# A 1024-wide trunk kernel: expert down weights loaded as two neighbouring rows per partition, with the gated rows transposed in steps of two

## The reference, cut to what matters

```python
D_MODEL, D_FF, N_EXPERTS, TOP_K = 1024, 3584, 8, 2
def swiglu(h, w_gu, w_down):
    g, u = jnp.split(h @ w_gu, 2, axis=-1)
    return (jax.nn.silu(g) * u) @ w_down
...
    for e in range(N_EXPERTS):
        out = out + combine[..., e:e + 1] * swiglu(h, w_gu[e], w_down[e])
```

## Time and profile before

| what | value |
|---|---|
| median of 3 runs | 1553.64 us |
| the profiled execution's own time | 1553.86 us |
| its span in the profile | 1552.1 us |
| mean granted clock of TensorE, of 1 | 0.994 |
| TensorE busy | 98% of the span |
| VectorE, ScalarE busy | 79%, 66% |
| main DMA queue, share of 16 engines | 77.5% |

### The profile page before, as it was taken

The page is one execution under the profiler, slowest core; times in us unless marked ns, Lnnn a source line. Parts: engine busy times, 40 slices in busy tenths (PEclk is TensorE's granted clock), DMA queues, the critical chain, the costliest instruction groups (busy, mean ns, idle before and its releaser), DMA issues.

```text
span 1552.1 us, 21140 instructions
## 1 busy us (share of the span) xinstructions
PE 1516.8 (98%) x7606; PEld 1276.4 (82%) x7606; DVE 1220.1 (79%) x1014; ACT 1023.6 (66%) x935; POOL 60.4 (4%) x98
## 2 busy tenths in 40 slices
PE   8899999999899999999999999999999999999997
PEld 7688888888899888788888888888888888888885
DVE  6664555456688758898898898898898998998896
ACT  5554444354678646877777777777777777776774
POOL 2052000000000002000000000000000000001020
PEclk9999999999999999999999999999999999999999
DMA  8369755546433338999999999999999999999997
GB/s 323 120 238 413 262 179 185 190 135 186 136 114 122 110 136 302 404 384 404 364 383 390 372 366 409 365 386 389 364 388 389 365 391 388 365 391 382 392 382 309
DMA packets 166230, 476.23 MB, mean 307 GB/s; under 512 B 9152, under 2 KB 35024, under 8 KB 166176
## 3 DMA queue, kind: packets, MB, share of 16 engines
q1 hardware_dynamic: 157152, 446.73, 77.5%
q0 software_dynamic: 5888, 19.23, 3.2%
q10 hardware_dynamic: 3136, 9.54, 1.5%
HBM read 454.49 MB, written 20.97 MB: 306 GB/s over the span
## 4 chain that ended last, share of the span: by engine, by line
PE 88%; DVE 5%; ACT 3%; DMA 2%; DVEq 1%; issue 1%; SPq 0%; ACTq 0%
PE bank L770 27%; PE bank L772 27%; PE bank L771 27%; PE bank L1223 2%; DVE acc L1666 1%; DMA ring<-swa_w_qkv_in 1%; DVE w_lo L1340 1%; DMA ring<-moe_w_gu_in 1%; ACT w_hi L447 0%; DVE w_lo L1728 0%; PE bank L1210 0%; PE bank L990 0%; PE bank L795 0%; ACT xs L620 0%; ACT L629 0%
## 5 line engine op out<-in xcount | busy, mean ns | idle before, releaser
L1728 DVE TENSOR_TENSOR w_lo<-ring,w_hi 128x2048 fp32r<-128x2048 f32 x336 | 763.0, 2289 | 79.0 <-PE bank L772 71.2
L664 ACT ACTIVATE w_hi<-ring 128x2048 fp32r<-128x2048 f32 x336 | 636.3, 1920 | 151.0 <-DMA ring<-moe_w_gu_in 101.7
L770 PE MATMUL bank<-w_hi,xgT_hi 128*128 128x512 f32 x896 | 351.2, 392 | 3.7 <-DVE w_lo L1728 2.6
L772 PE MATMUL bank<-w_hi,xgT_lo 128*128 128x512 f32 x896 | 349.0, 390 | 0.0
L771 PE MATMUL bank<-w_lo,xgT_hi 128*128 128x512 f32 x896 | 348.7, 389 | 0.0
L1340 DVE TENSOR_TENSOR w_lo<-ring,w_hi 128x2048 fp32r<-128x2048 f32 (+1 forms) x84 | 190.0, 2265 | 118.2 <-ACT w_hi L447 118.1
L447 ACT ACTIVATE w_hi<-ring 128x2048 fp32r<-128x2048 f32 (+1 forms) x84 | 158.9, 1897 | 121.7 <-PE bank L772 114.1
L770 PEld LDWEIGHTS bank<-w_hi,xgT_hi 128*128 128x128 f32 x896 | 168.2, 188 | 38.8 <-DVE w_lo L1728 3.4
L772 PEld LDWEIGHTS bank<-w_hi,xgT_lo 128*128 128x128 f32 x896 | 168.2, 188 | 35.3
L771 PEld LDWEIGHTS bank<-w_lo,xgT_hi 128*128 128x128 f32 x896 | 168.3, 188 | 34.1
L770 PE MATMUL bank<-w_hi,m_hT_hi 128*128 128x512 f32 x448 | 175.8, 392 | 0.0
(11 more groups left out here) (326 smaller groups left out, 1650.9 us busy)
## 6 DMA issues: line engine op xcount, KB each, us to landing
ring<-moe_w_gu_in SPq DMA_DIRECT2D x230, 1024.0 KB, 7.3
ring<-moe_w_down_in SPq DMA_DIRECT2D x112, 1024.0 KB, 7.0
ring<-ffn_w_gu_in SPq DMA_DIRECT2D x28, 1024.0 KB, 6.4
ring<-ffn_w_down_in SPq DMA_DIRECT2D x14, 1024.0 KB, 4.9
xg_rows<-zeros POOLq DMA_DIRECT2D x36, 256.0 KB, 12.4
ring<-ssm_w_in_in SPq DMA_DIRECT2D x8, 1024.0 KB, 4.9
ring<-ssm_w_in_in SPq DMA_DIRECT2D x16, 512.0 KB, 3.8
ring<-ssm_w_in_in SPq DMA_DIRECT2D x32, 256.0 KB, 4.3
```

Of the source, the lines that this page charges most:

```text
L664: act.activation(w_hi[:, c % HI], ring[:, c % RING], ACT.Copy).then_inc(hi_ready, 1)
L770: pe.matmul(o, stat[0], mov[0], start=start, stop=False)
L772: return pe.matmul(o, stat[1], mov[0], start=False, stop=stop)
L1728: dve.tensor_tensor(w_lo[:, c % SPLIT], ring[:, c % RING], w_hi[:, c % HI].bitcast(F32), ALU.subtract).then_inc(lo_ready, 1)
```

## The change

The load of a down chunk takes another view of the weights: partition p now gets rows 256c + 2p and 256c + 2p + 1, which lie beside each other in memory, 8 KB in one piece. So place k of chunk c holds row 256c + 2p + k. The transposes are cut to match: tile a of `f` takes columns of `m_hh` two apart, from column 256 (a // 2) + a % 2, instead of 128 neighbouring ones. Tile 2c + k then has hidden column 256c + 2p + k on partition p.

```diff
                     else:
                         n = D
-                        src = block_of(moe_w_down[0, e], 2 * (c - 4 * NJ), 2, 0, D)
+                        src = moe_w_down[0, e].rearrange("(c p k) n -> p c k n", p=P, k=2)[:, c - 4 * NJ]
                     dst = ring[:, c % RING, :].rearrange("p (k n) -> p k n", n=n)
                     sp.dma_start(dst, src).then_inc(slot_loaded[c % RING], 16)
...
                     for a in range(4):
-                        ins = pe.transpose(bank[4 + f % 2][:, a * P:(a + 1) * P], m_hh[:, f % 2, a * P:(a + 1) * P],
-                                           ident[:])
+                        of_tile = m_hh[:, f % 2].rearrange("p (c n k) -> p c k n", c=2, k=2)[:, a // 2, a % 2]
+                        ins = pe.transpose(bank[4 + f % 2][:, a * P:(a + 1) * P], of_tile, ident[:])
                     ins.then_inc(m_T, 1)
```

## The result

| | before | after |
|---|---|---|
| median | 1553.44 us (12 runs) | 1556.38 us (12 runs) |
| the profiled execution's own time | 1553.86 us | 1555.36 us |
| its span | 1552.1 us | 1553.6 us |
| ratio of times, 95% interval | 1 | 1.0019 [1.0011, 1.0026] |

The change makes the kernel 0.19% slower, some 2.9 us (1.7 to 4.0 by the interval). The forecast was 1553.6 us and no change; the time lies in the stated range (to 1556.5 us) and just inside the 0.2% that the prediction called no change, but the interval excludes 1. With twelve runs on each side a loss of this size can be told from none.

The account below looks back on a forecast made before the run. The prediction took TensorE to bound the kernel. Its three parts, each 0, added to the profiled 1553.86 us gave 1553.9 us, or 1553.6 us for the median: no change, range 1551.0 to 1556.5 us.

Parts of the forecast that it names:

- the added-up pass: In an expert pass, TensorE's matmuls, transposes and small lines sum to 118.3 us against 118.4 us measured, leaving nothing for waiting.
- Part 1, the 8 KB loads: Down loads in pieces of 8 KB: gain bounded by 2.6 us of TensorE's waiting, neither place reachable, so taken as 0.
- The room of 13 us a pass: DMA loads take 105.4 of a pass's 118.4 us; the 13 us left would hide slower down loads.
- Part 2, the stepped transposes: On TensorE, 224 transposes load m_hh elements 8 bytes apart: taken as 0, with 11.6 us as the far end.
- Rival A: Slower: TensorE loads the stepped tile's 128 columns at half rate or worse; 11.6 us more, 1565.2 us; chance 8%.
- The tell it named: Sign in the profile after that stepped weight loads cost time: eight transposes on TensorE taking over 0.98 us.
- Part 3, what reads the new layout: Copies, subtractions and all 504 matmuls of a pass read the same addresses as before: 0.
- B: Slower: DMA engines serve 8 KB pieces of down chunks worse; 36 us over 8 passes, 1590 us; chance 2%.
- C: Faster: fewer pieces free DMA engines and memory, quickening TensorE; 1551.0 us if all stalls went; chance of over 0.2%: 3%.
- D: The down load is cut again into 4 KB pieces on its way; time as forecast; chance 10%, inside "no change".

## Why the prediction was wrong

- **What bounds the kernel**: right. TensorE was and is busy for every microsecond of a pass, and the added-up pass leaves no place for a loss to hide. That is why 11 ns on an instruction that takes 2.7% of the chain can be seen at all. (One small misreading: the DMA engines read 7, not 9, in the last slice, in which the experts end.)
- **Part 1, the 8 KB loads**: right, 0. The load alone has the passes of before to the hundredth, and the packets fell by 14336, as foreseen. The room of 13 us a pass was never needed.
- **Part 2, the stepped transposes**: this is the step that failed, in "so I take 0". It excluded a gain rightly and set the ends at 0 and 11.6 us; the measured price is 2.5 us. The mistake was to take L1050 as the nearest row. That load reads one element 128 times in 189 ns, 3 ns less than a plain one of its kind, and it told nothing of a load that passes over every other element, which takes 209 ns in place of 140. There was no row on a stepped load, and the cost falls on the one engine without room; then 0 is a bound, and nothing made it the likeliest value. Rival A named the mechanism, with a chance of 8%, and oversized it more than fourfold: it took what was left of a transpose's 109 ns as the time of its load, 52 ns, and doubled it. In the runs the load's own record grows by 69 ns, by half and not to twice, and nearly all of that overlaps other work: 11 ns reach TensorE's time. The tell it named, over 0.98 us for eight, was set by that size too; 0.95 us was the answer.
- **The rule on SBUF lines** (the Trainium skill, Advanced Engine Details and Errata, section "SBUF Cachelines"): two hits on a line of 16 bytes are said to be enough for full rate. The traces disagree for a load of weights: a step of two has two hits and takes 209 ns in place of 140, and a step of four, with one hit, costs no more than 1 ns a transpose beyond it. The Trainium skill's neighbouring note on non-contiguous patterns is written of PSUM, which was written in order before and after, so no run here bears on it.
- **Part 3, what reads the new layout**: right, 0. TensorE's matmuls still start 0.227 us apart, and in the experts it waits for VectorE no more than before (2.3 us for `w_lo`, 2.6 before).
- **Rivals B, C and D**: none came. B would have shown TensorE waiting for down chunks, and D no fall in the packets.
- **The numbers**: the range held the time by 0.1 us, and that was luck: its upper end is a quarter of A's price, 2.9 us, and no row gave that quarter. The direction was missed, because "no change" got 87% where no row priced a stepped load on the bound engine. A loss of 0.19% could be told from none, though the prediction put the least that can be told at 0.2%.

## What to carry to other kernels

TensorE was busy for every microsecond of a pass, and an edit that added eleven nanoseconds to one of its instructions went straight into the time. So look at which operand of which instruction changes its pattern, and take zero only if a row shows that same pattern. Give the sorting to an engine with room: VectorE wrote the same order at 420 ns more a product, and the passes kept their length. The leaner transfer was worth nothing, since the engine it feeds did not wait for it in the passes.

## What the runs showed of the hardware

- LDWEIGHTS of 128 float32 columns for a transpose, in groups of four and eight, takes 140 ns in the median for neighbouring elements, 208 to 209 ns for every second, 198 ns for every third and 211 ns for every fourth. A load of every second element that stands alone behind matmuls of 512 columns takes 198 ns. In the groups the step costs TensorE 11.1, 5.4 and 11.8 ns a transpose for steps of two, three and four; three is the cheapest of them, which I can't explain.
- The price did not vanish behind longer matmuls: 8 to 10 ns a stepped transpose with three matmuls of 512 columns ahead of each.
- A transpose alone between products costs 0.119 us, in a group of eight 0.109 us.
- A load of 1 MB with 128 pieces of 8 KB (shape 128x2048) costs SyncE 333 ns to issue, one with 256 pieces of 4 KB (shape 128x2x1024) 373 ns; whether the pieces or the shape make the difference was not tried.
- VectorE's product of 512 columns grew from 680 to 1100 ns when it wrote neighbours 128 elements apart.
